# First projection's input tiles 1280 bytes apart, and weights whose place shifts a little with every chunk

## What is computed

```python
# first block, l = 0; h holds 16 meta tokens and 256 tokens
proj = h @ w_in[l]              # (272 x 2048) @ (2048 x 7176)
...
# second block
h = rms_norm_2(x, norm1_g[l]) * (1.0 + sc1[:, None]) + sh1[:, None]
proj = h @ w_in[l]              # (256 x 2048) @ (2048 x 8192)
```

## Time and profile before

| | before |
|---|---|
| median of three runs | 3518.31 us |
| the profiled execution's own time | 3518.49 us |
| its span | 3516.9 us |
| TensorE, matmuls | busy 3464.3 us (99%) |
| TensorE, weight loads | 3272.3 us (93%) |
| VectorE / ScalarE / GpSimd | 75% / 59% / 3% |
| HBM | 204 GB/s over the span |

### The profile page before, as it was taken

One profiled execution on the slowest core, in us unless ns is written; L12 is line 12 of the kernel. 1 busy time (PEld: TensorE's weight loads), 2 busy tenths in 40 slices (PEclk: granted clock), 3 DMA queues, 4 the chain that ended last, 5 costly groups with the idle time before them and its releaser, 6 DMA issues.

```text
span 3516.9 us, 75127 instructions
## 1 busy us (share of the span) xinstructions
PE 3464.3 (99%) x26793; PEld 3272.3 (93%) x26793; DVE 2648.1 (75%) x4912; ACT 2074.4 (59%) x3860; POOL 108.4 (3%) x169
## 2 busy tenths in 40 slices
PE   7999999999999999999999998999999999999999
PEld 7999999999999999787788887999999999999999
DVE  7775688788888888555588877999667687666555
ACT  5456655677767777455455556665565665555554
POOL 1000030000000000000000000000000000000000
PEclk9999999999999999999999999999999999999999
DMA  8854488555655555565788874555456556666555
GB/s 326 327 177 152 144 293 294 159 188 187 189 179 167 167 167 167 162 215 186 268 329 327 327 257 140 178 165 159 144 182 196 187 184 190 194 192 193 188 185 173
DMA packets 184771, 721.34 MB, mean 205 GB/s; under 512 B 20512, under 2 KB 23072, under 8 KB 171808
## 3 DMA queue, kind: packets, MB, share of 16 engines
q1 hardware_dynamic: 167328, 608.57, 53.2%
q0 software_dynamic: 14496, 103.82, 8.3%
q10 hardware_dynamic: 2784, 6.78, 0.5%
HBM read 714.89 MB, written 4.19 MB: 204 GB/s over the span
## 4 chain that ended last, share of the span: by engine, by line
PE 89%; DVE 6%; issue 3%; ACT 1%; DMA 1%; DVEq 0%; SPq 0%; ACTq 0%
PE PS L458 22%; PE PS L459 21%; PE PS L460 21%; PE PS L596 7%; PE PS L597 7%; PE PS L598 7%; PE PS L838 1%; DVE wlo L1872 1%; PE PS L887 0%; DMA raw<-peer_v_dram 0%; PE PS L689 0%; DVE big L1602 0%; DVE big L1923 0%; PE PS L637 0%; DVE big L1921 0%
## 5 line engine op out<-in xcount | busy, mean ns | idle before, releaser
L1026 ACT ACTIVATE whi<-raw 128x512 fp32r<-128x512 f32 x1832 | 1137.0, 629 | 998.8 <-PE PS L460 643.3
L1529 DVE TENSOR_TENSOR wlo<-raw,whi 128x512 fp32r<-128x512 f32 x1448 | 975.4, 690 | 551.8 <-ACT whi L1026 546.1
L458 PE MATMUL PS<-tok_parts_hi,whi 128*128 128x256 f32 x2048 | 578.3, 282 | 1.9 <-ACT big L1236 0.7
L459 PE MATMUL PS<-tok_parts_lo,whi 128*128 128x256 f32 x2048 | 570.5, 279 | 0.0
L460 PE MATMUL PS<-tok_parts_hi,wlo 128*128 128x256 f32 x2048 | 570.3, 278 | 0.0
L1675 DVE TENSOR_TENSOR wlo<-raw,whi 128x512 fp32r<-128x512 f32 x596 | 404.6, 695 | 151.8 <-ACT whi L1114 103.5
L1114 ACT ACTIVATE whi<-raw 128x512 fp32r<-128x512 f32 x468 | 292.0, 629 | 279.6 <-PE PS L460 278.3
L596 PE MATMUL PS<-whi,hhi 128*128 128x512 f32 x1024 | 404.3, 395 | 3.7 <-DVE wlo L1529 1.9
L597 PE MATMUL PS<-wlo,hhi 128*128 128x512 f32 x1024 | 404.2, 395 | 0.0
L598 PE MATMUL PS<-whi,hlo 128*128 128x512 f32 x1024 | 404.0, 395 | 0.0
L458 PEld LDWEIGHTS PS<-tok_parts_hi,whi 128*128 128x128 f32 x2048 | 386.1, 189 | 5.7 <-DVE wlo L1872 3.0
(11 more groups left out here) (522 smaller groups left out, 8045.6 us busy)
## 6 DMA issues: line engine op xcount, KB each, us to landing
raw<-peer_u_dram SPq DMA_DIRECT2D x256, 512.0 KB, 3.5
raw<-peer_v_dram SPq DMA_DIRECT2D x256, 512.0 KB, 3.9
raw<-w_in_dram SPq DMA_DIRECT2D x240, 512.0 KB, 3.6
big<-w_mod_dram POOLq DMA_DIRECT2D x96, 1024.0 KB, 5.2
raw<-w_up_dram SPq DMA_DIRECT2D x176, 512.0 KB, 3.6
raw<-w_down_dram SPq DMA_DIRECT2D x88, 512.0 KB, 4.3
raw<-w_out_dram SPq DMA_DIRECT2D x64, 512.0 KB, 3.8
raw<-w_query_dram SPq DMA_DIRECT2D x32, 512.0 KB, 4.9
```

What stands on the lines that cost most here:

```text
L458: pe.matmul(out, hi, rhi, start=start, stop=False, **more)
L459: pe.matmul(out, hi, rlo, start=False, stop=False, **more)
L1026: f(whi[:, m % PAIRS, quarter(q)], raw[:, m % RING, quarter(q)], ACT.Copy).then_inc(hi_ready, 1)
L1529: dv.tensor_tensor(wlo[:, m % PAIRS, quarter(q)], raw[:, m % RING, quarter(q)], whi[:, m % PAIRS, quarter(q)], ALU.subtract).then_inc(lo_r ...
```

## The change

- The arena grows to 2 x 16 x 320 floats. The first projection's input goes to new views `far_hi`, `far_lo`: the same tiles of 272 columns, now 1280 bytes apart. The low parts of all inputs in the arena begin 20480 bytes past the high ones (before: 17408). `hhi`, `hlo` stay 1088 apart for what peer_v keeps there.
- `in_parts` begins 320 bytes past the arena's start (before: 192).
- Each half of `whi` and `wlo` has room for 64 more floats. `walked` shifts the parts within it: by 4 x (23 - c) floats in chunks 8 to 23 of the first projection, by 4 x (39 - c) in chunks 24 to 39, by 63 - c floats in chunks 1 to 63 of w_in_2; elsewhere by 0. The shift falls by 16 bytes a chunk, and by 4.
- Where the shift rises from one chunk to the next (`moves_up`), six halves wait until the whole half before them in their place has been used.
- The first projection's splits are written half by half. POOL's descriptor scratch is halved to 8192 bytes per partition, which makes the room.

```diff
-        arena = sb("arena", [P, 2 * KC * KEYS])
+        arena = sb("arena", [P, 2 * KC * 320])
         hhi = nc.alloc_sbuf_tensor_at("hhi", [P, KC, KEYS], F32R, offset=at)
-        hlo = nc.alloc_sbuf_tensor_at("hlo", [P, KC, KEYS], F32R, offset=at + KC * KEYS * 4)
+        hlo = nc.alloc_sbuf_tensor_at("hlo", [P, KC, KEYS], F32R, offset=at + KC * 320 * 4)
+        far_hi, far_lo = (nc.alloc_sbuf_tensor_at("far" + part, [P, KC, 320], F32R, offset=at + k * KC * 320 * 4)[:, :, 0:KEYS]
+                          for k, part in enumerate(("_hi", "_lo")))
...
-            return [split_view(name + part, at + k * KC * KEYS * 4 + beyond, rows, row, SEQ)
+            return [split_view(name + part, at + k * KC * 320 * 4 + beyond, rows, row, SEQ)
...
-        in_hi_, in_lo_ = parts("in_parts", KC, 192)
+        in_hi_, in_lo_ = parts("in_parts", KC, 320)
...
-        whi = sb("whi", [P, PAIRS, HALF], F32R)
-        wlo = sb("wlo", [P, PAIRS, HALF], F32R)
+        whi_room = sb("whi", [P, PAIRS, HALF + 64], F32R)
+        wlo_room = sb("wlo", [P, PAIRS, HALF + 64], F32R)
+        whi, wlo = whi_room[:, :, 0:HALF], wlo_room[:, :, 0:HALF]
+
+        def walked(room, m, q=None, block=None):
+
+            c, c2 = (m - FIRST["w_in"]) // 2, (m - FIRST["w_in_2"]) // 2
+            shift = 63 - c2 if 1 <= c2 < 64 else 4 * (23 - c) if 8 <= c < 24 else 4 * (39 - c) if 24 <= c < 40 else 0
+            first, n = (q * HALF // 2, HALF // 2) if block is None else (block * P, P)
+            return room[:, m % PAIRS, shift + first:shift + first + n]
+
+        def moves_up(m):
+
+            return m - FIRST["w_in_2"] in (2, 3) or m - FIRST["w_in"] in (16, 17, 48, 49)
...
-                hi, lo = (t[:, :, KEYS - width:] for t in (hhi, hlo)) if name == "w_in" else (in_hi_, in_lo_)
+                hi, lo = (t[:, :, KEYS - width:] for t in (far_hi, far_lo)) if name == "w_in" else (in_hi_, in_lo_)
...
-                        last = three(PS[:, c % 2, 0:width], whi[:, half, at_], wlo[:, half, at_],
+                        m = h0_ + 2 * c + half
+                        last = three(PS[:, c % 2, 0:width], walked(whi_room, m, block=kc), walked(wlo_room, m, block=kc),
...
-                sc.wait_ge(quarters_used, 2 * m + q + 1)
-                f(whi[:, m % PAIRS, quarter(q)], raw[:, m % RING, quarter(q)], ACT.Copy).then_inc(hi_ready, 1)
+                sc.wait_ge(quarters_used, 2 * m + (2 if moves_up(m) else q + 1))
+                f(walked(whi_room, m, q), raw[:, m % RING, quarter(q)], ACT.Copy).then_inc(hi_ready, 1)
...
-                    split(0, FIRST["w_in"], 2 * c + 2)
+                    split_half(2 * c + 2)
+                    split_half(2 * c + 3)
...
-                dv.tensor_tensor(wlo[:, m % PAIRS, quarter(q)], raw[:, m % RING, quarter(q)],
-                                 whi[:, m % PAIRS, quarter(q)], ALU.subtract).then_inc(lo_ready, 1)
+                dv.tensor_tensor(walked(wlo_room, m, q), raw[:, m % RING, quarter(q)],
+                                 walked(whi_room, m, q), ALU.subtract).then_inc(lo_ready, 1)
...
-    nc = bacc.Bacc("TRN2", target_bir_lowering=False, num_devices=1)
+    nc = bacc.Bacc("TRN2", target_bir_lowering=False, num_devices=1, dynamic_dma_scratch_size=8192)
```

More of the change, by code:

```diff
@@ L232, in build @@
         rows_end = arena[:, 1088:3136].rearrange("p (b t i) -> p b t i", b=4, t=4)
-        cols_end = arena[:, 5440:7488].rearrange("p (b t i) -> p b t i", b=4, t=4)
+        cols_end = arena[:, 6208:8256].rearrange("p (b t i) -> p b t i", b=4, t=4)
         p2 = region(0, 64, SEQ)
@@ L1062, in split_input @@
                         continue
-                    f((hhi if o == 0 else at_hi)[:, base + k * group:base + (k + 1) * group, :], src[:, k * group:(k + 1) * group, :],
+                    f((far_hi if o == 0 else at_hi)[:, base + k * group:base + (k + 1) * group, :], src[:, k * group:(k + 1) * group, :],
                       ACT.Copy).then_inc(in_hi, 1)
@@ L1592, in low @@
                     if shift is None:
-                        dv.tensor_tensor(hlo[:, 4 * k:4 * k + 4, o:], h[:, 4 * k:4 * k + 4, :], hhi[:, 4 * k:4 * k + 4, o:],
+                        dv.tensor_tensor(far_lo[:, 4 * k:4 * k + 4, o:], h[:, 4 * k:4 * k + 4, :], far_hi[:, 4 * k:4 * k + 4, o:],
                                          ALU.subtract).then_inc(in_ready, 1)
```

## The result

The changed kernel took 3522.35 us (median of ten runs, 3517.11 to 3527.70), the kernel before, beside it on the same chip, 3515.51 us (ten runs, 3510.09 to 3522.85): a ratio of 1.0023, interval [1.0014, 1.0032]. It is slower by 6.8 us, where 3.8 us faster had been forecast. The profiled execution took 3517.11 us.

A forecast was written before the change was run, and what follows sets the result against it. TensorE, busy 99%, was taken as the bound: matmul count times distance between starts. Terms -7.6 + 3.5 + 0.3 = -3.8 us against 3518.5 gave 3514.7 us, range 3499 to 3529.

The forecast's parts named there:

- part 2: Walk of the weights: each offset keeps a chunk on one of two steps; second mixer 3.5 us more.
- 48 of 64 slow: Second mixer: 48 of 64 chunks on the slow step instead of 32, 3.5 us more.
- all slow: Second mixer: upper bound with every chunk on the slow step, 6.9 us more.
- Part 1: First projection's pitch of 1280 bytes: constant offset shortens matmul distances, 7.6 us less, between 2.8 and 13.6.
- Part 4: Splits as halves, halved POOL scratch, other tiles moved by multiples of 256 bytes: costs nothing.
- part 3: Six halves wait for the whole half before them: 0.3 us more, bounds 0 and 4.2.
- rival 2: Second mixer: weights beginning off a line cost a step, 120.0 ns; +10.0 us in all, 3528.5; chance 0.22.
- Rival 1: First projection and second mixer both lock on the fast step: -20.2 us, 3498.3; chance 0.20.
- Rival 3: Both stages: addresses do nothing, order and gaps alone set the step; 3518.5 us; chance 0.12.
- Rival 4: Untouched stages flip steps; the up projection turning slow would cost +13.8 us; chance 0.04.

The follow-up runs named there:

- e6: Changed kernel with the second mixer's weights moved by 32 bytes only every eighth chunk, eight chunks at each offset, first projection unshifted; 3539.05 us.
- e8: Changed kernel with offset 192 in every first-projection chunk but the first, second mixer as before; 3509.66 us, ratio 0.9988 to the kernel before.
- e5: Changed kernel with the second mixer's input at 320 and weights shifted by a constant 128 bytes, so offset 192 again; 3526.5 us.
- e1: Changed kernel without its address changes: pitch 1088, input at 192, no shift; 3520.18 us, ratio 0.9989 to the kernel before.
- e4: Changed kernel, second mixer's part alone, its walk in 16-byte steps every fourth chunk; 3528.68 us, ratio 1.0009 to the kernel before.
- e3: Changed kernel with the first projection back at pitch 1088 and unshifted, second mixer's part alone; 3521.72 us, ratio 0.9989 to the kernel before.
- e9: Changed kernel, unaltered, measured and profiled once more; 3522.04 us, ratio 1.0007 to the kernel before.
- e10: Kernel before the change, unaltered, profiled once more; 3511.28 us.

## Why the prediction was wrong, and where it was right

**What failed: part 2, "I take it that each offset still puts a chunk on one of the two steps".** The two steps are those of offset 192, the only one the second mixer had, and of 64. At most others the distances are different ones, from 116.6 to 123.4 ns (e6 and the walk), and 113.3 is rare. "48 of 64 slow" thus gave too little: the mean became 118.4 ns, above the slow step itself. The term was +3.5 us with an upper bound of +6.9 ("all slow"), and measured +8.1 by distances, +5.1 to +7.1 by the stage's length. The bound came from the two rows at 192 and wasn't a bound for offsets that no row showed, though the 258-column row (120.0) and the first projection's mix (118.3, above the slow step in the mean of four offsets) both pointed upward: a mean of 118.3 cannot be made of 113.3 and 117.8. The prediction quoted that mean and still rounded it down to the slow step.

**Part 1 was mis-sized the same way.** The base of 120.0 ns for 272 wide was the 258-column stage's. No chunk of 272 came below 123.3 in any kernel. Pitch alone gave 2.8 us, the lower bound; I had taken 7.6, and the walk there gave back 1.3, where the text called the offsets already in the midpoints. That the stage fetches densely took nothing: e8 ran at 123.4 with 361 GB/s. The prediction had called steps above 126 ns a proof that this base was wrong; chunks 10 to 12 have 126.3.

**What held.** With both addresses moved and the offset kept at 192, the two levels and their share stay (e5), which is what the prediction assumed; that the period is 256 and not more was tested by no other run. The plumbing is neutral in the two touched stages (e1). Part 4 put it at nothing everywhere, which isn't shown: peer_u is 2 to 4 us longer in every kernel that has it. The waits of part 3 cost 0 to 0.4 us, for 0.3 taken. No fetch came late, with the scratch halved: chunks 10 to 12 run without a pause at a DMA share of 0.95.

**The rivals.** The median, 3522.35 us, lies within the stated range, 3499 to 3529, but that is no credit to the sum: the range reached so high for rival 2's sake. Rival 1 needed the fast step everywhere: 4 of 63 chunks had it. Rival 2 got the sign and not the mechanism: it forecast 120.0 ns off a line, and e4 on lines is no faster than e3 (118.7 against 118.4 ns). The Trainium skill's lines of 16 bytes (SBUF — State Buffer, Door 1: The DMA port swizzle) therefore don't show here in where a weight load begins. Rival 3, addresses do nothing, falls by e6: eight chunks at 120.0, eight at 118.7, eight at 116.6 to 116.9 in one stage. The Trainium skill's page SBUF — State Buffer, Who interferes with whom, speaks of two independent read ports and of a TensorE that never waits on anyone. The prediction read from it that addresses are worth 0 us. The trace doesn't agree with that reading: 123.4 instead of 113.3 ns at full clock, by where the two operands lie. That the two reads hinder each other is my reading of it; the runs show only that the distances follow the offset. Rival 4, untouched stages flip, came true in part and got a chance of 0.04 on the ground that "the steps survive from run to run (2.4 us spread)". That was wrong: three runs had happened to agree. In four sets of runs the kernel before had medians of 3515.51, 3533.38, 3513.01 and 3519.71 us, and untouched stages stood on either step in different profiles (up projection 347.8 or 361.5 us from first to last start, w_query, w_out_2, down projection). Of these only w_query was seen on both in one and the same program. The measured change is small beside this. Its sign rests on ten runs of either kernel on the same chip; the repetition, e9, could not tell it from nothing.

**Why the sign came out.** By distances +8.1 us in the second mixer and -1.5 in the first projection; by length the second mixer alone is worth +5.1 to +7.1. To this come 2 to 4 us in peer_u, whose cause is open, and stages such as w_down, which in both profiled pairs gave 9 us back and whose step in the other runs nobody saw. The second mixer's part is shown; that the whole 6.8 us is made of the two touched stages is not. What the walk averages over was good already: 192 is the best of the eight offsets measured, and the kernel before had it in every 256-wide stage but the first projection.

## What to carry to other kernels

Where TensorE is the bound and each matmul has its own weight load, read the distance of starts for each address offset (moving less weights, modulo 256) before moving anything, and hold the best one; a walk over offsets gives their average. When a stage's mean lies between or above the steps one knows, there are further steps, and bounds from the known ones are no bounds. Small changes are judged inside the touched stage, on several profiles, and the untouched stages are looked through too: a total can flip its sign by them, and plumbing that seems neutral may lengthen one.

## What the runs showed of the hardware that was not expected

- The commonest distances have a grain: a group of three products takes 340.0, 353.3 and 360.0 ns at 113.3, 117.8 and 120.0 ns a matmul, which is 51, 53 and 54 times 6.667 ns, or 16 cycles at the 2.4 GHz that were granted. Others (116.6, 118.7, 123.4) are no whole multiples, so this is a pattern and not a rule shown. At 256 wide no chunk ran below 113.3 ns, at 272 wide none below 123.3.
- At offset 192 (and 64) two distances, 113.3 and 117.8, are both stable for hundreds of microseconds; a stage can start on either. Offset 208 has two as well, 118.4 and 123.4 (e4).
- The kernel before ran from 3505.01 to 3540.35 us in 79 runs, with a granted clock of 0.992 to 0.998. The two steps of untouched stages are large enough to make most of it (between profiles of different kernels 13.7 us for the up projection, 9.2 for the down projection).
- Short drops to half clock in the first projection, behind 180 us, differ from profile to profile: three in before and e9, one in e10, none in after and e1.
